# A hybrid encoder block on one core: the expert phase written out as 128 periods, with value sums one group behind the dots

## What is computed

```
qr = (xb @ w_query).reshape(BLOCK, HEADS, 2, 128)
s1 = einsum('thd,hnd->thn', qr[:, :, 0], keys1)
s2 = einsum('thd,hnd->thn', qr[:, :, 1], keys2)
v1, i1 = top_k(s1, 16);  v2, i2 = top_k(s2, 16)
cand = (v1[..., :, None] + v2[..., None, :]).reshape(BLOCK, HEADS, 256)
sc, ci = top_k(cand, 16)
eid = take_along_axis(i1, ci // 16) * 128 + take_along_axis(i2, ci % 16)
gate = softmax(sc)
hid = einsum('thkd,td->thk', expert_u[eid], xb)
act = gelu(hid) * gate
out = einsum('thk,thkd->td', act, expert_v[eid])
```

## Time and profile before

| | |
|---|---|
| median of 3 runs | 3868.45 us (3862.61 to 3877.56) |
| profiled execution, first to last instruction | 4090.1 us |
| PE busy | 3315.7 us (81%) |
| DVE busy | 2191.8 us (54%) |
| POOL busy | 2278.2 us (56%) |
| ACT busy | 992.4 us (24%) |
| moved by DMA | 1214 MB, of it 1073.87 MB by POOL's gathers |

### The profile page before, as it was taken

One profiled execution on the slowest core, in us unless ns is written; L12 is line 12 of the kernel. 1 busy time (PEld: TensorE's weight loads), 2 busy tenths in 40 slices (PEclk: granted clock), 3 DMA queues, 4 the chain that ended last, 5 costly groups with the idle time before them and its releaser, 6 DMA issues.

```text
span 4090.1 us, 38210 instructions
## 1 busy us (share of the span) xinstructions
PE 3315.7 (81%) x11032; PEld 1816.9 (44%) x11032; DVE 2191.8 (54%) x4881; ACT 992.4 (24%) x2278; POOL 2278.2 (56%) x2189
## 2 busy tenths in 40 slices
PE   8997757897788787887879778877888687969999
PEld 4444535453444344443535344444545253534444
DVE  1124285567444854477456744486357644574543
ACT  2112213222222132212221222212221222213332
POOL 0000055667556775767566755676566656666764
PEclk9998778898889897898889888898899798989999
DMA  3321187899789998899889978899799979999996
GB/s 125 118 75 63 39 298 263 309 363 389 264 302 335 362 358 289 316 346 365 280 313 373 365 269 297 318 360 342 278 324 369 356 260 322 352 364 373 381 355 243
DMA packets 413927, 1214.00 MB, mean 297 GB/s; under 512 B 43680, under 2 KB 137888, under 8 KB 413600
## 3 DMA queue, kind: packets, MB, share of 16 engines
q0 software_dynamic: 294912, 1073.87, 71.6%
q1 hardware_dynamic: 118816, 137.66, 9.9%
HBM read 1190.61 MB, written 20.77 MB: 296 GB/s over the span
## 4 chain that ended last, share of the span: by engine, by line
PE 54%; DVE 14%; issue 13%; DMA 7%; POOL 5%; ACT 4%; another core or an unknown queue 2%; SPq 1%; POOLq 0%; DVEq 0%; ACTq 0%
PE expert_sum L894 28%; PE bank L894 23%; DVE u_rows L1645 5%; DMA u_rows<-in_peer_u_dram,group_ids 4%; DMA w_query<-in_peer_w_query_dram 3%; PE bank L897 3%; POOL u_rows L576 3%; POOL v_rows L576 2%; ACT weight_diagonals L610 1%; ACT L610 1%; ACT arena L610 1%; DVE arena L1420 1%; DVE arena L1552 1%; DVE arena L1537 1%
## 5 line engine op out<-in xcount | busy, mean ns | idle before, releaser
L894 PE MATMUL expert_sum<-v_rows,weight_diagonals 128*128 128x512 f32 x4096 | 1871.7, 617 | 153.0 <-ACT weight_diagonals L610 116.9
L576 POOL DMA_INDIRECT v_rows<-in_peer_v_dram,group_ids x1024 | 1191.1, 1163 | 827.7 <-PE expert_sum L894 541.8
L1645 DVE CUSTOM_DVE_ANT_0 u_rows<-u_rows,ffn_in 128x1024 f32<-128x1024 f32 x1024 | 1215.7, 1225 | 454.8 <-DMA u_rows<-in_peer_u_dram,group_ids 410.3
L894 PEld LDWEIGHTS expert_sum<-v_rows,weight_diagonals 128*128 128x128 f32 x4096 | 810.4, 200 | 1161.7 <-issue 1078.0
L576 POOL DMA_INDIRECT u_rows<-in_peer_u_dram,group_ids x1024 | 1052.3, 1028 | 416.8 <-issue 371.0
L897 PE MATMUL bank<-constants,arena 128*128 128x128 f32 x968 | 184.5, 336 | 330.2 <-DVE arena L1475 82.4
L610 ACT ACTIVATE weight_diagonals<-constants,expert_weight 128x128 f32<-128x128 f32 x1024 | 331.7, 390 | 228.5 <-PE expert_sum L894 177.4
L894 PE MATMUL bank<-w_query,arena 128*128 128x256 f32 (+1 forms) x1088 | 297.6, 436 | 87.4 <-DMA w_query<-in_peer_w_query_dram 50.6
L610 ACT ACTIVATE gelu<-hidden 128x8 f32<-128x8 f32 x128 | 26.7, 208 | 1386.1 <-DVE hidden L1645 1237.0
L897 PEld LDWEIGHTS bank<-constants,arena 128*128 128x128 f32 x968 | 139.1, 171 | 392.6 <-issue 212.2
L894 PEld LDWEIGHTS bank<-w_query,arena 128*128 128x128 f32 x1088 | 231.6, 215 | 155.7 <-issue 59.6
(11 more groups left out here) (166 smaller groups left out, 1968.1 us busy)
## 6 DMA issues: line engine op xcount, KB each, us to landing
w_query<-in_peer_w_query_dram SPq DMA_DIRECT2D x64, 1024.0 KB
u_rows<-in_peer_u_dram,group_ids POOLq DMA_INDIRECT x1024
v_rows<-in_peer_v_dram,group_ids POOLq DMA_INDIRECT x1024
w_channel<-in_w_in_dram SPq DMA_DIRECT2D x12, 512.0 KB
conv_scratch<-conv_out SPq DMA_DIRECT2D x12, 512.0 KB, 2.6
arena<-conv_scratch SPq DMA_DIRECT2D x8, 768.0 KB
tok_scratch<-token_out SPq DMA_DIRECT2D x8, 648.0 KB
arena<-tok_scratch SPq DMA_DIRECT2D x8, 648.0 KB
```

Source lines behind the costliest of these rows:

```text
L576: nc.gpsimd.indirect_dma_start(ring[:, j, :], None, table, bass.IndirectOffsetOnAxis(ids[:, half, j:j + 1], 0)).then_inc(landed[j], 16)
L894: return nc.tensor.matmul(out_, lhsT, rhs, start=start, stop=stop, **kw)
L1645: v.tensor_tensor_reduce(u_ring[:, j, :], u_ring[:, j, :], xb[:], 1.0, 0.0, ALU.mult, ALU.add, hid[:, g * G + j:g * G + j + 1]).then_inc(u ...
```

## The change

The experts become 128 periods, q = 16 * tile + group, all straight code on every engine. In period q:

- DVE does the dots of group q, and after the first two of them the weights of group q-1 (`begin`). PE does the value sums of group q-1 and ACT the gelu and diagonals of q-1.
- The dots and the value sums are generators (`expert_dots`, `expert_slots`), and `fill(n)` takes the next n of them. Calls of `fill` stand in the front pieces ahead of the waits on other engines. What is left is done at the end of the period (`fill(G)`).
- POOL issues the 8 u gathers of group q, then the 8 v gathers of group q-1. At the start of a tile it issues the v gathers first, then takes the new expert numbers. `ids` gets 4 places instead of 2.
- The pieces are dealt anew to the 16 periods, two to a period in places (`front_piece`); pieces of PE stand at periods 0 to 12, those of DVE at 0 to 14.

The work of each kind is the same: 1024 u gathers, 1024 v gathers, 1024 dots, 2048 value matmuls, and the same front instructions. The rings keep 8 places each.

```diff
@@ gpsimd
-                for table, ring, used, landed in ((table_u, u_ring, u_used, u_landed), (table_v, v_ring, v_used, v_landed)):
-                    for j in range(G):
-                        if j % 2 == 0 and not first:
...
-                            pool.wait_ge(used, n - G + j + 2)
+            for q in range(NP):
+                e, g = divmod(q, NG)
+                late = g == 0 and e > 0
+                if late:
...
+                    for pair in range(G // 2):
+                        gather_v(q - 1, pair)
+                if late or q == EARLY:
+                    take_ids(e)
...
+                for pair in range(G // 2):
+                    gather_u(q, pair)
+                if q and not late:
+                    for pair in range(G // 2):
+                        gather_v(q - 1, pair)
@@ tensor
             def level(t, l):
...
+                fill(1)
                 for r in range(2):
                     pe.wait_ge(inv_ready, n + r + 1)
...
+                fill(1)
                 for r in range(2):
                     pe.wait_ge(level_x_out, n + r + 1)
...
+            def fill(n):
...
+                for _ in range(n):
+                    next(slots, None)
...
+            for q in range(1, (NT - 1) * NG):
+                slots = expert_slots(q - 1)
+                for i in front_piece(q):
+                    pieces[i](q // NG + 1)
+                fill(G)
@@ vector
             def level(t, l):
                 for r in range(2):
+                    fill(2 if r == 0 else 1)
                     dve.wait_ge(level_p, 10 * t + 2 * (l - 1) + r + 1)
...
+            def expert_dots(q):
                 for j in range(G):
-                    dve.wait_ge(u_landed[j], (t * NG + g + 1) * 16)
+                    dve.wait_ge(u_landed[j], (q + 1) * 16)
+                    col = (q % NG) * G + j
                     v.tensor_tensor_reduce(u_ring[:, j, :], u_ring[:, j, :], xb[:], 1.0, 0.0, ALU.mult, ALU.add,
...
+            def begin(q):
...
+                fill(2)
+                if q:
+                    expert_weights(q - 1)
+                e, g = divmod(q, NG)
+                if e and g == 0:
+                    publish_gate(e)
+                if e and g == 1:
+                    experts_out(e - 1)
...
+            for q in range((NT - 1) * NG):
+                dots = expert_dots(q)
+                begin(q)
...
+                for i in front_piece(q):
+                    pieces[i](q // NG + 1)
+                fill(G)
```

295 lines of the change are left out of this document (157 added, 138 removed).

## The result

| | before | changed |
|---|---|---|
| median | 3870.48 us (3862.61 to 3877.56, 4 runs) | 4326.02 us (4313.55 to 4334.54, 4 runs) |
| ratio, 95% interval | | 1.118 (1.115 to 1.121) |

The changed kernel is 456 us slower. I had forecast 3698 us, 172 us faster. Its profiled execution has a span of 4332.7 us.

The account below looks back on a forecast made before the run. Waits bound the loop tiles; afterwards POOL (371 us a tile) and a new chain would. Excess of 44 us gives 415 a tile, 30 less; six tiles save 180 us, scaled to 170: 3698 us, range 3540 to 3850.

Parts of the forecast that it names:

- The chain: Each period: last dot frees u places, first v gather follows, lands, value sums, piece steps, last dot; above 23.2 us it lengthens.
- The excess is 44 us, the tile 415 us: Loop tiles: periods whose chain exceeds 23.2 us add 44 us a tile, giving 415, 30 less than 445.6.
- rival 3: Front periods: later landing and half-clock PE make the new chain slower, 478 us a tile, 4050 us; chance 0.08.
- short chains or none: Periods 0, 6, 7 and 10 to 15: no excess over POOL's 23.2 us each.
- So the loop tiles lose time to waits, not to work: Six loop tiles at 445.6 us: no engine full, POOL waiting 541.8 us for PE, DVE 410.3 us for u rows.
- 0.946: Unprofiled over profiled time, 3868.45 / 4090.1; scaled the profile's 180 us gain to 170 us.
- my stalls of the loop: Waits at L1364 and L1432 on DVE, laid to the loop's taken branch; removing them saves some 15 us a tile.
- POOL is last: After the change POOL bounds the tile: sixteen gathers and ids copy, 23.2 us a period, 371 a tile; DMA 362, PE 354.
- A chance of 0.20 for 3525 us: Rival that the floor is reached: shorter chains, tiles near 371 to 395 us, 3525 us; chance 0.20 for 3450 to 3630.
- Costed at nothing: Generator order adds no instruction, ids copies stay 128, register arithmetic of waits goes: no cost for the new order.
- Rival 2: Waits only move, POOL to u, PE to v rows; only loop stalls go: 3783 us; 0.16 with mild Rival 4.
- Rival 4: Straight code is fetched late, stalls remain or multiply: 3783 us, or near 3868; strong form 0.06, mild shares Rival 2's 0.16.

Follow-up runs that it names:

- e14: Changed kernel with all eight dots of a group ahead of DVE's front piece, batch where before takes about 3870 us: 3922.5 us, ratio 1.016.
- e12: Kernel before with its loops written out, old order of work, batch where before takes about 3870 us: 3862.1 us, ratio 0.998.
- e2: Kernel before with its loops written out, same kernel as e12, in a batch of the longer kind: 4002.7 us, ratio 0.982.
- e13: Unrolled kernel before with only POOL's order changed: u gathers of a group, then v gathers of the group before: 3846.9 us, ratio 0.996.
- e4: Changed kernel with all eight dots ahead of DVE's front piece, same kernel as e14, in the longer kind: 4119.6 us, ratio 1.010.
- e8: Changed kernel with dots first, then GELU and weights of the same group in its own period: 4129.3 us, ratio 0.997.
- e18: Kernel of e17 with the old POOL order in the last tile alone: ratio 0.988.
- e3: Changed kernel with POOL's old order, v gathers of the group before ahead of u gathers: 5094 us, ratio 1.249.
- e7: Changed kernel with DVE's eight dots and PE's eight value sums ahead of their pieces, nothing spread: 4811 us, ratio 1.160.
- e9: Kernel of e8 with POOL's old order, v gathers of the group before ahead of u gathers: 5098 us, ratio 1.319.
- e11: Kernel of e3 with the weights of the group before moved ahead of the first two dots on DVE: 4483 us, ratio 1.158.
- e17: Kernel of e8 with the three lists of pieces of the kernel before (old dealing): ratio 0.991.

## Why the prediction was wrong

**The chain was right, its sum too short.** A level period was put at 28.0 us (8.8 for the gathers, 19.2 from PE's first value sum to DVE's last dot). Measured: 9.0 (2051.97 to 2060.97) and 21.2, so 30.2. The whole tile, with periods taken from the weights of one group (L1686) to those of the next, in us, mean of the six tiles:

| periods | my sum | changed kernel | e14, chain cut |
|---|---|---|---|
| 1 to 8 | 223.8 | 252.5 | 206.4 |
| 9 to 14 | 142.2 | 163.7 | 155.4 |
| 15 and 0 | 49.4 | 55.6 | 48.8 |
| tile | 415.4 | 471.8 | 410.7 |

(The 3 us that my sum gives back in period 9 are counted with period 8; cut at the copy, the tiles are 471.7 and 409.0.) The term that failed is "The excess is 44 us, the tile 415 us": over the floor of 371 us it was 101. In periods 1 to 8 the chain itself is longer than I added it. One value sum at half clock and the longer landing are what I had named in rival 3 and left out of the forecast. Period 5 takes 36.9 us against 29.2; period 7, which I had among those with "short chains or none" at 23.2, takes 31.4, and 22.4 in e14, so it had the chain too. In periods 9 to 14 the 23.2 us were no floor of any order: even e14 takes 155.4 there. Rival 3 put its deciding point at 32.5 us on average for periods 1 to 8; they take 31.6. The landing was taken from the row and not from the rule (Trainium skill, DMA: Bandwidth & Descriptors, Anatomy of one DMA; an estimate of 3.2 us by its figures), and there the row was right: 5.5 us from issue to use.

**The other step that failed is the baseline.** "So the loop tiles lose time to waits, not to work", at 445.6 us a tile: in the executions by which the result is measured a tile has 409.4 us (e12), at a DMA share of 0.95 to 0.96. I noticed that profile and runs were 5.7% apart and made a factor of it, 0.946, in place of asking whether the excess was in the very waits that I was about to remove. It was: of the 36 us between 445.6 and 409.4, 15 by my sum were my stalls of the loop, and they have nothing to do with the loop (e2, e12).

**With it the floor was wrong.** "POOL is last" with 371 us, and 362 us for the DMA by 402 GB/s: no middle tile of any kernel came under 405. At 407 to 409 us the DMA moves 354 to 358 GB/s with a share of 0.96 to 0.97 (e12, e14). The 402 GB/s of the earlier trace rows were 25 us of a full queue, not a rate for a tile. A chance of 0.20 for 3525 us rested on that.

**What each cost.** The changed kernel takes 628 us more than the 3698 that I forecast. In the trace, before any factor, it has 4332.7 us against the 3910 that I added up, 423 more: some 340 in the six tiles, 65 in the last, 21 in tile 0. The other 205 come from the factor. With the right baseline alone, my 415 us a tile would be some 3890 us beside e12's 3856, no gain; the size of the loss is the chain's.

**"Costed at nothing" hid a wait.** The weights and GELU of a group go a period later while PE, which was one group behind already, stays where it is. I checked that no instruction was added and did not ask who stands ahead of GELU on ACT: a piece that waits for PE. It shows in the query periods and in the last tile. A query period:

```profile
2288.44 6.74 PE L894 MATMUL bank<-w_query,arena 128*128 128x256 f32 x16 [5.13 <-DMA w_query<-in_peer_w_query_dram]
...
2303.68 0.21 ACT L615 ACTIVATE gelu<-hidden 128x8 f32<-128x8 f32 x1
...
2303.92 0.17 DVE L1686 TENSOR_TENSOR expert_weight<-gelu,gate 128x8 f32<-128x8 f32 x1 [13.18 <-ACT gelu L615]
```

Weights 13.18 us behind GELU, GELU behind copies that wait for PE, and PE for the query weights (5.13 us). Periods 9 to 14 take 163.7 us together, where I had 142.2, but the late weights aren't needed to explain it: e12, which has them in time, takes 161 to 165 there (by where one cuts the period), and e14, which has them late, 155.4. In the last tile they do show. There I said that it keeps its time (435.5 us in the trace of before, 430.3 in e12), and it is 500.4. e14, with the chain cut and the weights late, still has 496.9; POOL's order alone makes 448 of 430 (e13), and the other 49 us are left for the late weights. That is a subtraction; the direct pair, e4 to e8, gives 32 us (505 to 473) in executions of the longer kind. And e18, with early weights and the old POOL order there, still has 463.0, against 433.5 in e2 of the same kind: some 30 us of the last tile have no cause yet.

**Tile 0**, "no difference, within 20 us", lost 33 by its end against e12; in e14, without the chain, it lost 2.5 (971.99 against 969.46).

**The rivals.** Rival 3 had the mechanism and the sign, with 0.08 and 4050 us. On e12's scale, 409.4 a tile, the same sum (478 a tile) would have given 3870 + 6 by 69 = 4280 us. Rival 2 saw POOL's wait move from v to u, which it did. Rival 4: no sign of late code in the changed kernel's trace, nor in e12's, whose PE stands 0.5 us for nothing.

**The whole in parts.** From e12 to the changed kernel are 477 us of span. From e12 to e14, with everything but the dots' place, are 67: 2.5 up to the first copy at L1674, -2.4 in the six tiles, 66.6 from the last copy on. From e14 to the changed kernel are 410: 30 in tile 0, 376 in the six tiles (471.7 against 409.0), 4 at the end. So 86% of the loss are dots that stand behind steps of the front, and 14% the last tile, of which the late weights are the larger part by subtraction. The loops (e12) and POOL's order in the middle tiles (e13) are worth nothing either way. These parts hold in this order only: e3, e7, e9 and e11 show that each undone by itself breaks another.

What stays open: what makes the longer kind of execution, what the dealing costs by itself, what holds the last tile of e18, and whether e17 or e18 is faster than the kernel before in the shorter kind.

## What to carry to other kernels

When the profiled span and the timed runs are some per cent apart, the excess may lie in just the waits that one is about to remove: price a gain against the rows that would be there in the timed runs, and take a floor in absolute time, not scaled. When work is moved a step later on one engine, list for each moved instruction what now stands ahead of it, and draw the ring (free place, gather, landing, sum, step, dot, free place) before counting its slack: work that frees a buffer belongs ahead of waits on other engines, not among them. Two orders that each look worse may need each other (spread value sums and late v gathers), so an experiment that undoes one of them measures the broken pair; read its trace before its time.

## What I had not expected of the hardware

- The same program takes 3862 and 4003 us on the same chip in two batches (e12, e2), with all timed runs of the kernel before in a batch at one level. In the longer kind PE stands for nothing that the trace shows (108 us in e2, 0.5 in e12) and other engines wait for it, put down to "remote" (221 us against none).
- In one group of a level, the 32 matmuls of a level step took 5.46 us in e2 and 3.88 in e12, at the same place of the program. The granted clock of that stretch was 0.69 in e2 and 1.00 in e12, though in the 10.4 us ahead of it PE had the same instructions, the same busy time and a clock of 1.00 in both:

```profile
2355.51 5.46 PE L894 MATMUL bank<-arena 128*128 128x128 f32 x32 [1.13 <-ACT arena L714]
2345.00:2355.40 10.40, 8.06 (x50) 4.99 (x48) 4.45 (x7) 3.17 (x10) 7.07 (x9) 1.00 0.91 317
2355.50:2361.00 5.50, 5.46 (x32) 5.27 (x32) 0.73 (x1) 1.62 (x3) 3.98 (x5) 0.69 0.90 304
```

```profile
2273.51 3.88 PE L894 MATMUL bank<-arena 128*128 128x128 f32 x32 [1.13 <-ACT arena L714]
2263.00:2273.40 10.40, 8.05 (x50) 4.99 (x48) 4.44 (x7) 2.92 (x10) 6.91 (x9) 1.00 0.93 328
2273.50:2277.40 3.90, 3.88 (x32) 3.69 (x32) 0.73 (x1) 1.61 (x3) 2.98 (x4) 1.00 0.96 333
```

- A middle tile with its 256 gathers took 405 us or more in every kernel (358 GB/s at a share of 0.97 in the tile of e14 above), though single stretches of 25 us reach 402 GB/s.
- A gather keeps POOL longer when a dot runs on DVE beside it: in the trace of the changed kernel 1.48 us on average for the 575 gathers that had a dot beside more than half of their first 0.94 us, 0.96 us for the 1173 that had none (e12: 1.37 and 0.97).
